# The adaLN modulation at the start of a two-block transformer kernel: first part by single-column matmuls, inputs in three parts instead of four

## The reference, cut to what matters

```python
cs = jax.nn.silu(c)                                   # (1, 2048)
mod = cs @ w_ada[l] + b_ada[l]                        # (2048 x 12288)
sh1, sc1, gt1, sh2, sc2, gt2 = [m[:, None, :] for m in jnp.split(mod, 6, axis=-1)]
h = _rmsnorm(x, g_pre_mix[l]) * (1.0 + sc1) + sh1
proj = h @ w_in[l]                                    # (2048 x 11344)
...
x = x + gt1 * _rmsnorm(y, g_post_mix[l])
h = _rmsnorm(x, g_pre_ffn[l]) * (1.0 + sc2) + sh2
```

## Time and profile before

| | |
|---|---|
| median of 3 runs | 2658.14 us (2656.03 to 2658.14) |
| the profiled execution | 2658.12 us |
| its span, first to last instruction | 2656.3 us |
| PE busy | 2556.4 us, 96% |
| DVE busy | 1749.3 us, 66% |
| ACT busy | 1207.9 us, 45% |
| DMA, mean over the span | 213 GB/s, 567.10 MB |
| first matmul of the input projection | 45.34 us after the span's start |

### The profile page before, as it was taken

The page is one execution under the profiler, slowest core; times in us unless marked ns, Lnnn a source line. Parts: engine busy times, 40 slices in busy tenths (PEclk is TensorE's granted clock), DMA queues, the critical chain, the costliest instruction groups (busy, mean ns, idle before and its releaser), DMA issues.

```text
span 2656.3 us, 30340 instructions
## 1 busy us (share of the span) xinstructions
PE 2556.4 (96%) x12208; PEld 2107.8 (79%) x12208; DVE 1749.3 (66%) x2407; ACT 1207.9 (45%) x1753; POOL 6.6 (0%) x16
## 2 busy tenths in 40 slices
PE   3999999999998999999999989999999999999998
PEld 2777777787776888888888878878778888888887
DVE  6788898988886876556556564546655465564555
ACT  3533445343446534434434455455554444443443
POOL 0000000000000000000000000000000000000000
PEclk9999999999999999999999999999999999999999
DMA  7777445778885676555555535533445555555553
GB/s 297 294 274 295 162 171 209 273 295 325 342 316 196 264 289 229 195 190 180 200 183 183 205 136 189 190 127 143 176 157 190 190 188 192 190 182 199 186 195 143
DMA packets 78412, 567.10 MB, mean 213 GB/s; under 512 B 8736, under 2 KB 8864, under 8 KB 9792
## 3 DMA queue, kind: packets, MB, share of 16 engines
q1 hardware_dynamic: 76896, 555.99, 57.5%
q0 software_dynamic: 1376, 9.17, 0.9%
HBM read 563.02 MB, written 2.10 MB: 213 GB/s over the span
## 4 chain that ended last, share of the span: by engine, by line
PE 79%; DVE 10%; ACT 3%; DMA 2%; issue 1%; DVEq 0%; ACTq 0%
PE ps L798 17%; PE ps L795 17%; PE ps L796 17%; PE ps L839 15%; PE ps L841 8%; DVE wl L1395 4%; DMA raw<-stream_in 2%; DVE ACC L1410 2%; ACT wh L1054 1%; PE ps L851 1%; ACT M L1176 1%; PE ps L1000 1%; DVE TMP L1528 1%; DVE M L1532 1%; PE ps L863 0%
## 5 line engine op out<-in xcount | busy, mean ns | idle before, releaser
L1395 DVE TENSOR_TENSOR wl<-raw,wh 128x1024 fp32r<-128x1024 f32 x851 | 1002.7, 1220 | 560.8 <-ACT wh L1054 560.5
L1054 ACT ACTIVATE wh<-raw 128x1024 fp32r<-128x1024 f32 x851 | 851.6, 1049 | 754.8 <-PE ps L798 523.7
L839 PE MATMUL ps<-HT,wh 128*128 128x512 f32 x1792 | 634.3, 399 | 0.0
L798 PE MATMUL ps<-wl,U 128*128 128x512 f32 x1376 | 537.7, 391 | 5.6 <-DVE wl L1395 5.6
L795 PE MATMUL ps<-wh,U 128*128 128x512 f32 x1376 | 539.5, 392 | 0.0
L796 PE MATMUL ps<-wh,U 128*128 128x512 f32 x1376 | 536.2, 390 | 0.0
L841 PE MATMUL ps<-HT,wl 128*128 128x256 f32 x1792 | 503.5, 281 | 0.5 <-DVE wl L1395 0.5
L795 PE MATMUL ps<-wh,HT 128*128 128x512 f32 x1120 | 451.5, 403 | 23.4 <-ACT wh L1054 10.6
L798 PE MATMUL ps<-wl,HT 128*128 128x512 f32 x1120 | 443.1, 396 | 6.2 <-DVE wl L1395 5.9
L796 PE MATMUL ps<-wh,HT 128*128 128x512 f32 x1120 | 439.7, 393 | 0.0
L839 PEld LDWEIGHTS ps<-HT,wh 128*128 128x128 f32 x1792 | 336.7, 188 | 83.0 <-DVE M L1769 0.2
(11 more groups left out here) (230 smaller groups left out, 1317.8 us busy)
## 6 DMA issues: line engine op xcount, KB each, us to landing
raw<-stream_in SPq DMA_DIRECT2D x527, 1024.0 KB, 4.8
M<-rows_in POOLq DMA_DIRECT2D x6, 1024.0 KB, 5.1
X<-x_in POOLq DMA_DIRECT2D x1, 2048.0 KB, 16.0
y_out<-X SPq DMA_DIRECT2D x4, 512.0 KB, 2.6
raw<-stream_in SPq DMA_DIRECT2D x1, 640.0 KB, 3.5
raw<-stream_in SPq DMA_DIRECT2D x1, 512.0 KB, 3.5
CT<-consts_in POOLq DMA_DIRECT2D x1, 376.0 KB, 7.0
CAUS<-masks_in POOLq DMA_DIRECT2D x1, 192.0 KB, 17.2
```

The costliest lines, as they stand in the source:

```text
L798: ins = e.matmul(o, ah, L[:, c:c + bw], start=False, stop=end)
L839: e.matmul(o[:, :], H[:, c], a.rearrange("p h n -> p (h n)"), start=k == 0, stop=False)
L1054: e.activation(H, raw[n % RAW][:, c:c + w], ACT.Copy).then_inc(*hi.tick(p))
L1395: e.tensor_tensor(L, raw[n % RAW][:, c:c + w], H.bitcast(F32), ALU.subtract).then_inc(*lo.tick(p))
```

## The change

x is loaded by two DMAs of 1 MB each on SP's queue, ahead of the stream. The 16 blocks of h are taken in three parts of 4, 5 and 7 (`PHASES`), not four of 4. The shift and scale of the first four blocks come from eight events of a new kind "p" (1 MB: all 2048 rows by 128 columns of sh1 or sc1), which PE multiplies itself: 16 fp32 matmuls an event with the 128 by 128 square of w_ada as the stationary operand and one column, silu(c), as the moving one. The order is: four "p" events (blocks 0 and 1), the first chunk of qi, four "p" events (blocks 2 and 3), the second chunk. The "s" events now have one block of rows each and the columns of 5 or 7 blocks of sh1 and sc1 (1280 or 1792 wide), 16 events each; all of them are placed in the first two parts. Their sums over the partitions, and those of sh2 and sc2, are taken with `ACC` as stationary operand, one column out per matmul (10, 14 or 8 matmuls), so that DVE reads them as columns and the diagonals go away. The transposes of x come in tiles of two blocks (one, where a part has an odd number), each with its own scaling by ACT, where before one scaling served four blocks.

```diff
+PHASES = (0, 4, 9, 16)
+X_TILES = [(k, min(2, k1 - k)) for k0, k1 in zip(PHASES, PHASES[1:]) for k in range(k0, k1, 2)]
...
-    for q in range(3):
-        mixed([f"{n}@{q}" for n in FIRST], [("s", q + 1, j) for j in range(8)], (1, 2, 3, 5, 6, 7, 9, 10))
-    mixed(["qi@3", "kiwi", "qB@3", "kB@3", "vB@3", "kA@3", "vA@3"], [], 1)
+    columns = [("s", q, k) for q in (1, 2) for k in range(16)]
+    chunks = phase(0)
+    for j in range(2):
+        out += [("p", 2 * j + i, part) for i in range(2) for part in range(2)]
+        if j == 0:
+            out.append(chunks.pop(0))
+    beside(chunks, columns, (1, 2, 2, 1, 2, 2, 2, 2, 2, 1, 1))
+    beside(phase(1), columns, (1, 1, 1, 1, 1, 0, 1, 1, 1, 1, 1, 0, 1, 1, 1, 1, 0, 0))
+    mixed(["qi@2", "kiwi", "qB@2", "kB@2", "vB@2", "kA@2", "vA@2"], [], 1)
...
-        return [("w_ada", 2 * i + t, D * part + 512 * name, 512) for t in range(2) for part in range(2)]
+        k0, k1 = PHASES[name:name + 2]
+        return [("w_ada", i, D * part + 128 * k0, 128 * (k1 - k0)) for part in range(2)]
+    if kind == "p":
+        return [("w_ada", k, D * i + 128 * name, 128) for k in range(16)]
...
-    while events[at["pos"]][0] == "s":
-        if at["pos"] == 5:
-            add("xnorm")
-        for m in ada(at["pos"]):
-            colsum(m)
-        at["pos"] += 1
-    drain()
+    add("xnorm")
+    add("matvec", 0)
+    add("xturn", 0)
+    add("xturn", 1)
+    for n in (1, 2, 3):
+        add("matvec", n)
+    add("mods", 0)
+    add("xhalves", 0)
+    split(4)
+    for t in range(2):
+        for b in range(2):
+            add("bank", "qi@0", parts[4], t, b, True, False)
+    at["done"] = parts[4][-1]
+    for n in (5, 6, 7, 8):
+        add("matvec", n)
+    add("mods", 1)
+    add("xhalves", 1)
+    at["pos"] = 9
...
         e.dma_start(VT[:, :], vecs).then_inc(vec_in, 16)
+        for t in range(2):
+            e.dma_start(X[:, t, :], x_in[0, 128 * t:128 * t + 128, :]).then_inc(x_landed[t], 16)
...
+                elif events[m][0] == "p":
+                    e.wait_ge(*matvec(m))
...
-        e.dma_start(X[:, :, :], x_in.rearrange("a (t p) n -> p (a t) n", p=128)).then_inc(x_landed, 16)
...
+        def mat_vec(n):
+            _, j, part = events[n]
+            b, c = 4 + 3 * (j // 2), 2 * part + j % 2
+            e.wait_ge(*silu("c"))
+            e.wait_ge(landed[n % RAW], 16 * (n // RAW + 1))
+            for k in range(16):
+                ins = e.matmul(bank[b][:, c:c + 1], raw[n % RAW][:, 128 * k:128 * k + 128], VT[:, V_C + k:V_C + k + 1],
+                               start=k == 0, stop=k == 15)
+            ins.then_inc(*matvec.tick(n))
...
+            if not by_rows(n):
...
+                for j in range(acc_width(n) // 128):
+                    ins = e.matmul(bank[4][:, j:j + 1], ACC[:, 128 * j:128 * j + 128], ONES[:, 0:1], start=True, stop=True)
...
-            for i in range(2):
-                e.wait_ge(*colsum((n, i)))
-                for j in range(4):
-                    ins = e.tensor_tensor_reduce(TMP[:, 128 * j:128 * j + 128], bank[4 + i][:, 128 * j:128 * j + 128],
-                                                 idn, 1.0, 0.0, ALU.mult, ALU.add, SUM[:, 4 * i + j:4 * i + j + 1])
```

On ACT the scaling of a tile of x now comes right before the tile's own halves:

```diff
+        def x_turn(p):
+            k, nk = X_TILES[p]
+            e.wait_ge(*stat("rx"))
+            if p > 1:
+                e.wait_ge(*turned(("turnx", p - 2)))
+            for t in range(2):
+                e.activation(x_part(p, t), X[:, t, 128 * k:128 * k + 128 * nk], ACT.Identity,
+                             scale=RS[:, t:t + 1]).then_inc(*xq.tick((p, t)))
...
+        def turn_x(task, seg):
+            x_turn(task[1])
+            k = X_TILES[task[1]][0]
+            e.wait_ge(*mods(("av", 1, max(q for q in PHASES if q <= k))))
+            float_out(task, seg, lambda k: AV[:, 1, k:k + 1], lambda k: AV[:, 0, k:k + 1])
```

More of the change, by code:

```diff
@@ L84, in plan @@
 def plan():
-    out = [("s", 0, j) for j in range(8)]
+    out = []
     def mixed(slabs, other, every, skip=0, avoid=False):
@@ L98, in mixed, with beside, phase @@
                     continue
-                if other and (n in every if isinstance(every, tuple) else n > 0 and n % every == 0):
+                if other and n > 0 and n % every == 0:
                     out.append(other.pop(0))
         assert not other
-    for q in range(3):
-        mixed([f"{n}@{q}" for n in FIRST], [("s", q + 1, j) for j in range(8)], (1, 2, 3, 5, 6, 7, 9, 10))
-    mixed(["qi@3", "kiwi", "qB@3", "kB@3", "vB@3", "kA@3", "vA@3"], [], 1)
+    def beside(chunks, other, counts):
+        for c, n in zip(chunks, counts):
+            out.append(c)
+            for _ in range(n):
+                out.append(other.pop(0))
+    def phase(q):
+        return [("g", f"{n}@{q}", i) for n in FIRST for i in range(len(slab_chunks(f"{n}@{q}")))]
+    columns = [("s", q, k) for q in (1, 2) for k in range(16)]
[6 more added lines that the diff above has]
+    beside(phase(1), columns, (1, 1, 1, 1, 1, 0, 1, 1, 1, 1, 1, 0, 1, 1, 1, 1, 0, 0))
+    assert not columns
+    mixed(["qi@2", "kiwi", "qB@2", "kB@2", "vB@2", "kA@2", "vA@2"], [], 1)
     ada = [("a", c, j) for c in (3 * D, 3 * D + 1024, 2 * D, 2 * D + 1024, 4 * D, 4 * D + 1024) for j in range(8)]
@@ L280, in colsum @@
         if events[n][0] == "s":
-            later("turnx", events[n][1])
+            for p, (k, _) in enumerate(X_TILES):
+                if PHASES[events[n][1]] <= k < PHASES[events[n][1] + 1]:
+                    later("turnx", p)
     def flush():
@@ L719, in turn_keys @@
         if kind == "turnx":
-            return [("h", 0, 4 * task[1] + k + i, t) for i in range(2) for t in range(2)]
+            return [("h", 0, k + i, t) for i in range(X_TILES[task[1]][1]) for t in range(2)]
         if kind == "gm":
@@ L727, in turn_keys, with by_rows, acc_width, mods_key @@
         return [("h", task[1] + 1, k + i, t) for i in range(2) for t in range(2)]
+    def by_rows(n):
+        return events[n][0] == "a" and events[n][1] // D in (2, 5)
+    def acc_width(n):
+        kind, q, _ = events[n]
+        return 256 * (PHASES[q + 1] - PHASES[q]) if kind == "s" else 1024
+    def mods_key(n):
+        kind, c, _ = events[n]
+        return ("av", 1, PHASES[c]) if kind == "s" else ("av", c // D - 1, c % D // 128)
+    def x_part(p, t):
+        k, nk = X_TILES[p]
+        return (QKT, RT)[t][:, 256 * (p % 2):256 * (p % 2) + 128 * nk]
     def products_of(c):
@@ L868, in pair @@
                 free[b] = [(scaled, (*task, seg))]
+        def x_turn(p):
+            (k, nk), b = X_TILES[p], 5 + p % 2
+            e.wait_ge(const_in, 16)
+            for s, q in free[b]:
+                e.wait_ge(*s(q))
+            for i in range(nk):
+                for t in range(2):
+                    e.wait_ge(*xq((p, t)))
+                    ins = e.transpose(bank[b][:, 256 * i + 128 * t:256 * i + 128 * t + 128],
+                                      x_part(p, t)[:, 128 * i:128 * i + 128], idn)
+            ins.then_inc(*turned.tick(("turnx", p)))
+            free[b] = [(halves, ("h", 0, k + nk - 1, 1))] if p < 2 else [(scaled, ("turnx", p, 0))]
         def turn_x(task, seg):
-            e.wait_ge(const_in, 16)
-            pair(task, seg, lambda t, k: (QKT, RT)[t][:, 128 * k:128 * k + 128], lambda t, k: (xq, (task[1], t)))
+            x_turn(task[1])
         def turn_u(task, seg):
@@ L1037, in tensor @@
                 column_sums(*what)
+            elif kind == "matvec":
+                mat_vec(*what)
+            elif kind == "xturn":
+                x_turn(*what)
             elif kind == "turn":
@@ L1074, in float_out @@
                 e.wait_ge(*tmp[0][0](tmp[0][1]))
-            for i in range(2):
+            nk = X_TILES[task[1]][1] if task[0] == "turnx" else 2
+            for i in range(nk):
                 kw = dict(scale=scale(k + i))
@@ L1079, in float_out, with x_turn, x_halves @@
                 ins = e.activation(TMP[:, 256 * i:256 * i + 256], bank[b][:, 256 * i:256 * i + 256], ACT.Identity, **kw)
-                ins.then_inc(*scaled.tick((*task, seg) if i else (*task, seg, "first")))
+                ins.then_inc(*scaled.tick((*task, seg) if i == nk - 1 else (*task, seg, "first")))
             e.wait_ge(*scaled((*task, seg)))
-            f = TMP[:, :].rearrange("p (k n) -> p k n", k=2)
+            f = TMP[:, 0:256 * nk].rearrange("p (k n) -> p k n", k=nk)
             e.activation(d[:, :, 0, :], f, ACT.Copy).then_inc(*high.tick(key))
             tmp[0] = halves, turn_keys(task, seg)[-1]
[L1086 to L1101, removed]
+        def x_turn(p):
+            k, nk = X_TILES[p]
+            e.wait_ge(*stat("rx"))
+            if p > 1:
+                e.wait_ge(*turned(("turnx", p - 2)))
+            for t in range(2):
+                e.activation(x_part(p, t), X[:, t, 128 * k:128 * k + 128 * nk], ACT.Identity,
+                             scale=RS[:, t:t + 1]).then_inc(*xq.tick((p, t)))
+        def x_halves(p):
```

(14 more changed lines are left out.)

118 lines of the change are left out of this document (60 added, 58 removed).

## The result

The changed kernel takes 2732.81 us in the median (2731.91 to 2736.8, 4 runs) against 2658.14 us: a ratio of 1.0286 with a 95% interval of 1.0268 to 1.0303. It is 75 us slower. The direction was forecast, with 2688 us; the time lies 35 us above the end of the range. In front of the lines of the changed kernel stand new numbers: its matvecs are L908, the three matmuls of a bank L852, L853 and L855, the split L1147 (ACT) and L1489 (DVE), w_ada L1507, the additions into M L1824, the transposes of x L955.

What follows compares the result with a forecast made beforehand. It took the head as bound by data and a serial chain, the next 220 us by DVE near its limit, the rest by PE. Head +26, w_ada parts +5, sums -1 made +30 on 2658.12: 2688 us, range 2648 to 2698.

Steps and rivals of the forecast that it cites:

- the head: Start of the kernel to chunk 2: eight matvecs on PE at the low clock delay the stream, +26 us.
- that cold start: Chunk 2 in the head: PE starts again at the low clock, 7 x 0.2 = 1.5 us.
- The price of a matvec: One "p" event on PE, 32 passes: 6.8 us at the low clock, 3.4 us at the full clock.
- The first rival: Matvecs in the head: passes of 0.107 us whatever the clock, or PE at 2.4 GHz; 2664 us, chance 0.25.
- The second, a cheap pass: Matvecs in the head: one-column passes cost 0.053 us, so DMA paces the head; 2650.5 us, chance 0.20.
- The third, 10 us an event: Matvecs in the head: load and pass one after the other at the low clock; 2710 us, chance 0.05.
- the parts with w_ada: First two parts: 147 us of DVE work at 84 to 88% busy, +2 to +10 us, taken as +5.
- its 25 us: Kernel before, 48 to 269 us: 25 us of PE time lost to a DVE near its limit.
- The bound of +10: Upper end for the two parts with w_ada, from DVE busy 84%: 175 us, 34 us lost against 23.8 before.
- The chain of x tiles: Part boundaries: ACT scales each x tile only after the previous tile's halves; some 3 us each, hidden or not.
- The sums as columns: Four "a" sums: PE gains nothing, DVE loses eight diagonals a sum; -1 us, between 0 and -4.

Runs made afterwards that it cites:

- e1: Changed kernel with four parts of 4 blocks and two-block w_ada events again, keeping the new head and sums as columns: 2689.98 us, ratio 1.0110.
- e5: Changed kernel with 45 extra fp32 matmuls of 128 columns on PE ahead of the first matvec: 2729.34 us (one run).
- e6: Changed kernel with each matvec cut to the last of its 16 matmuls, so results are not the reference's: 2691.33 us, ratio 1.0128.
- e3: Changed kernel with seven raw buffers instead of three until the last part begins: 2691.57 us, ratio 1.0116.
- e4: Kernel before the change with seven raw buffers instead of three until its last part begins: 2648.02 us, ratio 0.9956.
- e7: Changed kernel with ACT scaling the next tile of x ahead of this tile's halves, inside a part: 2722.8 us, ratio 1.0248.
- e8: Kernel before the change with only the sh1, sc1, sh2 and sc2 sums taken as columns, diagonals on DVE gone: 2656.29 us, ratio 0.9994.
- e2: Changed kernel with the first four blocks' modulation summed by DVE again, keeping the three parts and narrow events: 2695.99 us, ratio 1.0132.

## Why the prediction was right or wrong

**Right: the head.** The prediction had +26 us, measured 25.6 at matmul 24 and some 30 (e1) once chunk 2 had left the low clock. Its +1.5 for that cold start was too small. The price of a matvec, 6.8 us from the load's rows, was measured at 6.83, and the full-clock price, 3.4, by the steps of 0.112 us in e5: 32 of them make 3.6. The first event landed at 13.5 us, not 11.8; chunk 1 at 45.2, not 42 to 44; chunk 2 at 80.6, against 79.4. The first rival, whose sum the Trainium skill's rule gives too (TensorE: Matmul & The Clock Gate, LDWEIGHTS), falls for matvecs at the low clock. The Trainium skill's formula there gives 0.107 us for a load of 128 columns and names no clock; by it a matvec would be 3.4 us, an estimate. The trace has near that at the full clock (3.6) and 6.83 at a granted clock of 0.50. The second, a cheap pass, is what e6 imitates and exceeds: the head gains 13 us there, and the kernel is still 33 us slower. The third, 10 us an event, falls with the 6.83.

**Wrong: the parts with w_ada.** The step "at the 84% of before that is 175 us, at 88% 168 ... I take +5" measured about +48. It priced the two parts by DVE's work and a busy share carried over, as if DVE's rate were what bounds them. The work was right (147 us forecast, 59 + 82 = 141 measured from 82 to 290 us), the share was not. The runs showed another bound in its place: with three buffers a chunk waits for its own round trip of 9.2 us. DVE did the same work at 86% busy once there were seven buffers (e3), and 69% with three. Of the 48 us, 31 are waits for buffers that the change adds; most of the rest lies at the second boundary and in the first part, by e3 and e4. The hint stood in the earlier trace rows: of DVE's idle time ahead of the low halves all 16.9 us ended with ACT, whose own wait was not looked up. In the kernel before, from 48 to 269 us, it reads:

```profile
ACT wh L1054 <- DMA raw<-stream_in: 82.2, 21, 10.0
```

ACT is not the bound, so its wait alone proves nothing, but it asks why the data were late. e4 answered it: more buffers give the kernel before 10.6 us too, so its 25 us were not lost to DVE alone, as the prediction read them. The prediction also checked SP's waits in the head alone, though the change made the events narrower (640 and 896 KB for 1 MB) and twice as many, so that each held a buffer for less work. The bound of +10 was taken from the same ratio, not from another mechanism, and so was no bound. The direction came out as forecast through the head; this step had only the sign right, and a tenth of the size.

**The chain of x tiles** was named but put "within the ends"; e7 shows it worth 10 us with three buffers. There it is a part of the 48.

**The sums as columns**: -1 forecast, -2 measured (e8), which cannot be told from none.

Open: e1 and e2 add up to 70 of 75 us; what the 5 us between are was not followed. Nor was it tried apart whether the narrow events or their order beside the chunks does more.

## What to carry to other kernels

Before pricing a stretch by an engine's busy share, follow one buffer of the stream around: landing, first use, last use, next issue. With N buffers the round trip (here 9.2 us with three) must be no longer than the work that the bounding engine finds in N events in a row (here 5.45 us); smaller pieces in a fixed number of buffers hold less work and make it worse. What more buffers give back must be set against what they give the kernel before (41 and 10.6 us here). A matvec of 16 fp32 matmuls of one column costs 32 weight loads, 6.83 us at the low clock to which it falls here; summing on an idle DVE was cheaper than on an idle PE.

## What the runs showed of the hardware that was not expected

- Back-to-back weight loads with one-column matmuls count as PE busy at 100% and the granted clock still goes from 0.97 (10 to 20 us, dense matmuls) to 0.50 (22 to 42 us) in e5. Their passes start 0.112 us apart at the full clock and 0.213 at the low one.
- The profile gives a granted clock of 1.00 for stretches before the first change that it records: from 22 to 42 us e5 stands at 0.50 and the changed kernel, which has no warm-up, at 1.00, though a matvec takes 6.83 us in both. There the steps between instructions tell the clock, the view does not.
- In the changed kernel a narrow event of 640 KB lands 3.5 us after its issue with nothing else in flight (issued at 71.17 us), one of 1 MB 4.7 us (issued at 42.61). With three in flight, from 110 to 129 us, both kinds take 5.3 to 6.5 us.
- In e3 busy DMA engines move 358 GB/s where most rows are of 5 KB and 422 where few are.
